# Two-layer mLSTM/convolution/MoE trunk: gate rows summed and rows spread by GpSimd, head norm weight as a column, layer 2's router loads and last modulation units moved

## The reference, cut to what matters

```
cond = silu(c)
for l in range(2):
    mod = cond @ w_ada[l] + b_ada[l]
    sh1, sc1, gt1, sh2, sc2, gt2 = split(mod, 6)
    u = x * (1 + sc1) + sh1
    proj = u @ w_in[l]                       # q k v o, gates, conv b c h
    h = mlstm_chunkwise(q, k, v, i_pre, f_pre)
    h = head_norm(h, mh_norm_w[l]) * sigmoid(o)
    y_conv = short_gated_conv(cb, cc, ch, w_conv[l])
    mix = concat([h, y_conv]) @ w_out[l]
    x = layer_norm(ALPHA * x + (1 + gt1) * mix, ln1_g[l], ln1_b[l])
    u = x * (1 + sc2) + sh2
    y = hier_moe(u, ...)                     # 16 experts in 4 groups, 2 per token
    x = layer_norm(ALPHA * x + (1 + gt2) * y, ln2_g[l], ln2_b[l])
```

## Time and profile before

| | us |
|---|---|
| median of 3 runs | 819.16 |
| lowest, highest | 817.65, 821.26 |
| profiled execution, its own time | 819.95 |
| its span, first to last instruction | 818.1 |

### The profile page before, as it was taken

One profiled execution on the slowest core, in us unless ns is written; L12 is line 12 of the kernel. 1 busy time (PEld: TensorE's weight loads), 2 busy tenths in 40 slices (PEclk: granted clock), 3 DMA queues, 4 the chain that ended last, 5 costly groups with the idle time before them and its releaser, 6 DMA issues.

```text
span 818.1 us, 9332 instructions
## 1 busy us (share of the span) xinstructions
PE 790.1 (97%) x3834; PEld 425.7 (52%) x3834; DVE 425.1 (52%) x916; ACT 96.0 (12%) x217; POOL 28.7 (4%) x72
## 2 busy tenths in 40 slices
PE   7999999999999999999979999999999999999994
PEld 2585588465344434434337658856634444443431
DVE  0289889787413332341356995676741343334135
ACT  2211000012011101101121101001201100110110
POOL 3000000520000000000001000000000000000000
PEclk9999999999999999999999999999999999999998
DMA  9999999899999999999998799547799999999991
GB/s 311 389 387 339 387 388 361 323 361 365 413 409 415 416 409 414 415 409 414 415 386 302 287 385 386 190 184 286 294 409 409 415 415 409 415 415 410 414 414 68
DMA packets 90826, 299.34 MB, mean 366 GB/s; under 512 B 4172, under 2 KB 4476, under 8 KB 82588
## 3 DMA queue, kind: packets, MB, share of 16 engines
q1 hardware_dynamic: 87132, 291.62, 91.7%
q0 software_dynamic: 2592, 7.04, 2.3%
q10 hardware_dynamic: 1056, 0.03, 0.1%
HBM read 297.63 MB, written 1.05 MB: 365 GB/s over the span
## 4 chain that ended last, share of the span: by engine, by line
PE 84%; DMA 6%; DVE 5%; issue 3%; ACT 1%; POOL 1%; DVEq 0%; POOLq 0%
PE bank L696 23%; PE bank L652 17%; PE bank L720 12%; PE bank L683 8%; PE bank L669 7%; DMA ring<-in_w_up_dram 6%; PE bank L742 4%; PE bank L889 3%; PE bank L536 2%; DVE bench L1141 1%; PE bank L551 1%; PE bank L568 1%; PE bank L704 1%; PE bank L750 1%; DVE expo L1141 1%
## 5 line engine op out<-in xcount | busy, mean ns | idle before, releaser
L652 PE MATMUL bank<-uT,ring 128*128 128x256 f32 x640 | 140.7, 380 | 0.0
L652 PEld LDWEIGHTS bank<-uT,ring 128*128 128x128 f32 x640 | 120.9, 190 | 19.3 <-issue 3.6
L696 PE MATMUL bank<-ring,uT 128*64 128x512 f32 x448 | 99.2, 594 | 1.8 <-DMA ring<-in_w_up_dram 1.8
L720 PE MATMUL bank<-ring,hb 128*64 128x512 f32 x448 | 99.6, 595 | 1.4 <-ACT hb L1012 1.4
L696 PE MATMUL bank<-ring,qT 128*64 128x512 f32 x448 | 99.4, 594 | 0.2 <-issue 0.2
L1141 DVE SCALAR_TENSOR_TENSOR bench<-ring,cond,bench 128x512 f32<-128x512 f32 x126 | 94.7, 752 | 4.5
L1376 DVE SCALAR_TENSOR_TENSOR kT<-bank,share,gate_row 128x512 f32<-128x512 f32 x32 | 24.0, 749 | 90.0 <-PE bank L720 90.0
L683 PEld LDWEIGHTS bank<-ccT,X 128*128 128x128 f32 x512 | 61.5, 197 | 11.3 <-issue 11.3
L696 PEld LDWEIGHTS bank<-ring,uT 128*64 128x64 f32 x448 | 31.6, 137 | 64.6 <-issue 60.0
L683 PE MATMUL bank<-ccT,X 128*128 128x128 f32 x512 | 64.3, 284 | 0.0
L720 PEld LDWEIGHTS bank<-ring,hb 128*64 128x64 f32 x448 | 30.9, 137 | 62.8 <-issue 60.5
(11 more groups left out here) (278 smaller groups left out, 658.5 us busy)
## 6 DMA issues: line engine op xcount, KB each, us to landing
ring<-in_w_gate_dram SPq DMA_DIRECT2D x28, 2048.0 KB, 18.5
ring<-in_w_up_dram SPq DMA_DIRECT2D x28, 2048.0 KB, 19.6
ring<-in_w_down_dram SPq DMA_DIRECT2D x28, 2048.0 KB, 16.9
ring<-in_w_ada_dram SPq DMA_DIRECT2D x23, 2048.0 KB, 18.2
ring<-in_w_in_dram SPq DMA_DIRECT2D x14, 2048.0 KB, 17.9
ring<-in_w_out_dram SPq DMA_DIRECT2D x4, 2048.0 KB, 15.5
bench<-in_w_gate_dram SPq DMA_DIRECT2D x4, 2048.0 KB, 11.9
bench<-in_w_up_dram SPq DMA_DIRECT2D x4, 2048.0 KB, 18.7
```

The costliest lines, as they stand in the source:

```text
L652: last = pe.matmul(bank[4 + (b0 + q) % 4][:, 0:SEQ], w[:, kc, q * P:(q + 1) * P], uT[:, kc, :], start=(kc == 0), stop=(kc == KC - 1))
L696: last = pe.matmul(bank[bk][CAP * j:CAP * (j + 1), :], xg[b][:, 4 * h + k, CAP * j:CAP * (j + 1)], ring[s[h]][:, 4 * j + k, :], start=(h = ...
L720: last = pe.matmul(bank[6 + half][CAP * j:CAP * (j + 1), :], hhT[:, f, CAP * j:CAP * (j + 1)], ring[s[h]][:, 4 * j + 2 * i + half, :], sta ...
```

## The change

- `gate_row_half`, `gate_rows` and `gate_row_2` are gone. DVE adds 1/128 on each partition when it weighs a gate unit, so that the sum over partitions has the 1 in it. GpSimd's new `gate_half` waits for the unit to be weighed, adds the bias row to partition 0 of the partial sums with an accumulating DMA of 2 KB, waits for it, and runs one `partition_all_reduce` of 128x512, which leaves the gate row on all partitions. Gate 2's row has a place of its own, `gate_moe`, over `v_ext`, whose columns of ones GpSimd writes again for layer 1 (PE waits for `ones_back`).
- `norm_rows` loads `ln_g` and `ln_b` to one partition (4 KB each) and spreads them with `partition_broadcast`; the router biases likewise. Layer 0's first norm rows are now loaded right after the constants.
- The head norm weight comes in with the convolution weights as columns (one more small DMA on SP, 16 instead of 12 columns transposed) and is applied by ACT as the scale of its copy of the transposed heads, in four instructions of 128x256 instead of two of 128x512; DVE's multiplication of 128x1024 is gone, and so is `mh_w`.
- PE runs `four_columns` after the first piece of the output projection; where gate 2's matmuls stood it runs `stay_busy(4, 4)`, four bf16 matmuls of zeros.
- Layer 1's router loads (ten DMAs) move from layer 0's output projection to after layer 1's `x_full`. In layer 1 units 10 and 11 are loaded before projections 5 and 6, and DVE weighs them in the middle of the mixer; it waits there for `gate_row_ready` at 4l+1 and 4l+2.
- The first load into `bench` waits for `moe_sum`, for `gate_row_ready` at 4l+4 and, in layer 0, for `early_sum`.

```diff
@@ STREAM[1]
-                  ("proj", 1, 3), ("ada", 1, 8), ("ada", 1, 9), ("proj", 1, 4), ("proj", 1, 5), ("proj", 1, 6), ("ada", 1, 10),
-                  ("ada", 1, 11), ("wout", 1, 0), ("wout", 1, 1)]
+                  ("proj", 1, 3), ("ada", 1, 8), ("ada", 1, 9), ("proj", 1, 4), ("ada", 1, 10), ("ada", 1, 11), ("proj", 1, 5),
+                  ("proj", 1, 6), ("wout", 1, 0), ("wout", 1, 1)]
@@ sync
-                            sp.wait_ge(row_ext, 4 * l + 4)
+                            sp.wait_ge(moe_sum, l + 1)
+                            sp.wait_ge(gate_row_ready, 4 * l + 4)
+                            if l == 0:
+                                sp.wait_ge(early_sum, 1)
@@ gpsimd
+            def gate_half(l, which, half):
+                i = (GATE1, GATE2)[which] + half
+                sums = weighed_sums(l, i)
+                bias = b_ada[l, ADA_COL[i]:ADA_COL[i] + COLS].rearrange("(a n) -> a n", a=1)
+                pool.wait_ge(weighed, turn(l, i))
+                pool.dma_start(sums[0:1, :], bias, accum_op=ALU.add).then_inc(bias_added, 16)
+                pool.wait_ge(bias_added, 16 * (4 * l + 2 * which + half + 1))
+                row = (gate_row, gate_moe)[which]
+                pool.partition_all_reduce(row[:, half * COLS:(half + 1) * COLS], sums, P,
+                                          bass.bass_isa.ReduceOp.add).then_inc(gate_row_ready, 1)
...
             for l in range(DEPTH):
                 if l:
                     pool.wait_ge(x_full, l)
-                arrived(pool, "proj", l, 4 if l == 0 else 1)
-                load_gate_row(l, 0)
-                load_head_weight(l)
+                    pool.memset(v_ext[:, :, :, DK:DK + 1], 1.0).then_inc(ones_back, 1)
+                    load_route(l)
+                norm_rows(l, 0)
+                for half in range(2):
+                    gate_half(l, 0, half)
                 if l == 0:
                     arrived(pool, "wout", l, 1)
-                load_norm_rows(l, 0)
-                if l == 0:
-                    for i in range(DEPTH):
-                        load_route(i)
-                    for i in range(1, DEPTH):
-                        load_gates(pool, i)
-                pool.wait_ge(x_ready, 2 * T * l + T)
-                load_gate_row(l, 1)
+                    load_route(l)
+                    load_gates(pool, 1)
+                pool.wait_ge(route_landed, 16 * 10 * (l + 1))
+                pool.partition_broadcast(b_route_row[:, l, :], b_route_row[0:1, l, :], channels=P).then_inc(route_spread, 1)
+                pool.wait_ge(pv_done, HEADS * (l + 1))
+                for half in range(2):
+                    gate_half(l, 1, half)
                 pool.wait_ge(seeded, l + 1)
-                load_norm_rows(l, 1)
+                norm_rows(l, 1)
@@ vector
-                link(dve.tensor_tensor(hb[:, :, :], hb[:, :, :], mh_w[:, :].unsqueeze(1).to_broadcast([P, T, WM]), ALU.mult))
                 dve.tensor_tensor(hb[:, :, :], hb[:, :, :], o_sig[:, :, :], ALU.mult).then_inc(h_ready, 1)
...
-                gate_rows(l, 0)
-                for i in (GATE2, GATE2 + 1):
-                    dve.wait_ge(row_ext, 4 * l + 2)
-                    ada_weigh(l, i)
-                    if i == GATE2:
-                        moe_shift_scale(l)
                 dve.wait_ge(gate_row_ready, 4 * l + 2)
+                if l == 0:
+                    ada_weigh(l, GATE2)
+                moe_shift_scale(l)
+                if l == 0:
+                    ada_weigh(l, GATE2 + 1)
                 first_norm(l)
```

114 lines of the change are left out of this document (51 added, 63 removed).

## The result

The changed kernel takes **827.7 us** (median of 4 runs, 827.1 to 833.3) where the kernel before took 819.7 beside it: 1.0094 of its time, 95% interval 1.0061 to 1.0126. Forecast were 814.4 us and "faster", so the sign is wrong. The time lies inside the range, but through a cause that the range wasn't built on. The profiled execution has a span of 826.5 us, against 818.1: 8.4 us to find.

The account below looks back on a forecast made before the run. PE, with work for 97% of the span, was taken as the bound, the DMA weight stream close behind. Savings 1.8 + 0.95 + 0.2 + 1.8 = 4.75 us gave 814.4 us; range for 8 in 10: 812.5 to 830.

Parts of the forecast that it names:

- PE, gate 1's matmuls, -1.8: Output projection, layer 1: gate 1's matmuls go and four transposes move behind the first piece, saving 1.8 us.
- DVE, layer 0, -0.95: Layer 0's output projection: DVE loses the gate rows but waits 2 us for transposed sums, saving 0.95 us, not 3.
- rival 3: Layer 0's norm and routing: GpSimd's sums stretch DVE by a fifth, 2 to 3 us, giving 817 us; chance 0.08.
- PE, gate 2's matmuls, -0.1 a layer: Gate 2 on PE: four zero matmuls of about 1 us replace matmuls whose second lasts 1.10; saves 0.1 us a layer.
- DMA, -1.8: Expert weight stream: two row loads a layer go, so PE's two waits for the last up loads go, saving 1.8 us.
- the margin of 1.5 us: Expert weight stream: what is left of the DMA saving after PE's two waits are gone, 1.5 us.
- Costs at nothing: Head weight, extra small DMA, early norm rows, GpSimd code loading and layer 1's moved units: each priced at no loss.
- The new cost, GpSimd's sums: Gate sums and bias DMAs on GpSimd: layer 0's first `bench` load is free at 189.0, in time before 191.4.
- X = 5.1 us: GpSimd's time for one 128x512 sum over partitions, taken as a halving tree of eight passes of 0.64 us.
- Rivals 1, 2 and 4: Stream waits for GpSimd, 825.8 us (0.24); part comes back, about 819 (0.22); sums far slower, about 1135 (0.03).
- the sum's 4.75 us: Whole kernel: total saving forecast, 1.8 + 0.95 + 0.2 + 1.8 us.

Follow-up runs that it names:

- a_pe2_late: a_back with layer 1's first norm rows spread later and gate 2 summed by PE, not GpSimd, and copied by ACT: 817.4 us (0.9955).
- a_back: The changed kernel with one iota of four numbers at the end of GpSimd's stream: 819.4 us (0.9999 of the kernel before).
- a_pe2_fill: a_pe2_late with layer 1's norm rows back in place and eight filler matmuls on PE ending layer 0's experts: 815.7 us (0.9920).
- b_fill: The kernel before with eight filler matmuls on PE at the end of layer 0's experts, nothing else: 819.2 us (0.9972).
- b_sums: The kernel before with four unused GpSimd sums of a dead tile in layer 0 and an iota ending GpSimd's stream: 826.8 us (1.0061).
- b_spread: The kernel before with one unused row of four numbers spread over the partitions at the end of GpSimd's stream: 832.0 us (1.0163).

## Why the prediction was wrong

Point by point, in its own order:

- *PE, gate 1's matmuls, -1.8*: right. Layer 1's mixer went from 118.49 to 116.78, -1.71, both at full clock; in four later profiles of the changed family a clock dip takes it back.
- *DVE, layer 0, -0.95*: the mechanism right, with the wait for the transposes at 2.00 us where 2 were forecast, and the size right (-0.89 in a_pe2_late). In the changed kernel it did not come, since rival 3, given 0.08, stood in its place: DVE's operations beside GpSimd's sums. Rival 3 was thought of as a stretch by a fifth over 16 us. It is a hold of up to 2 us at a time on operations between SBUF tiles that start beside a sum: here 1.3 us ahead of X's first norm, and 0.5 us behind it. "Layer 0: -0.95 us" became +0.44.
- *PE, gate 2's matmuls, -0.1 a layer*: -0.25 in layer 0 and 0 in layer 1 (from X's first norm to the first `share`, 35.79 to 35.54 and 35.61 to 35.61). The 35.54 has a clock dip in it, 188 to 192, where PE waits for DVE; a_back has 35.49 without one.
- *DMA, -1.8*: the mechanism right, the size nearer to -1.1. In the changed kernel's own profile the last pair of layer 0 begins 1.24 us earlier behind the one ahead of it (25.38 to 24.14), that of layer 1 0.48 (25.16 to 24.68), together -1.7. But that profile is one of the two best of its family. PE's two waits for the last up load together are 1.6 to 1.9 us in the six profiles of the kernel before's family (mean 1.75) and 0.25 to 1.3 in the eight of the changed family (mean 0.7). So they shrink and don't go, and the margin of 1.5 us that the prediction saw behind them isn't there. On the way to softmax 1 the changed kernel then loses 0.8 us, with PE idle for 4.46 us instead of 4.07 and a longer dip of the clock behind it.
- *Costs at nothing*: **this is the step that failed.** The prediction put "the code that GpSimd's new operations may have to load" at nothing, since "GpSimd is free from 8 us". That prices the load where the new operations stand, and there it does cost nothing (6.63 us of idle time, hidden). The load that costs, if that is what the idle time is, is that of the old operations: the constants' code, which the kernel before always found in place. It costs 10.46 us ahead of PE's first matmul with a constant, and all behind it is as late. In the profile of before nothing shows it, because that kernel holds operations of one kind; what was left out is that a profile shows one execution in a row of them.
- *The new cost, GpSimd's sums*: X = 5.1 us was too high, 3.24 measured, and the bias DMA 5.2 to 5.4 instead of 6.2; both harmless. Rivals 1, 2 and 4 fell with it: no wait of the stream for GpSimd was found. The 62 us for 512 columns that the rate in the Trainium skill, page "GPSIMD Engine Reference", section 3.2, would give are 19 times what this operation takes.

With the start put right (a_back) the changed kernel equals the one before, and with gate 2's sums away from DVE as well (a_pe2_late) it is 0.45% faster. What stays open is how much of that, a_pe2_fill over b_fill included, is the sum's 4.75 us: the rows give 0.9 + 1.7 + 0.2 + 1.1 = 3.9 us, the medians 3.6 (a_pe2_fill against b_fill) and 3.8 (a_pe2_late against the kernel before). That the forecast range held the measured 827.7 is luck: it reached that far for a stream that waits for GpSimd, and the stream didn't.

## What to carry to other kernels

Ask of a GpSimd operation of a new kind not only what it costs where it stands, but what it leaves loaded for the next execution: here one unused row at the end of the stream cost 1.6%, and one iota behind it gave that back. Put GpSimd's work on SBUF where DVE idles or reads PSUM, not where DVE is the engine that ends last; a sum that is off the path itself can still hold DVE's instructions that are on it. And where savings of a microsecond are at stake, compare stretch by stretch, with the granted clock beside each, since a dip of the clock is as large as any of them.

## What the runs showed of the hardware that I had not expected

- GpSimd's change of kind (a load of code, as inferred above): 10.6 to 10.7 us of idle time ahead of the first select of an execution whose kernel ends with a partition operation; 10.9 to 12.9 us ahead of an iota behind a partition operation; 6.1 us (b_sums) to 9.8 us (a_pe2_late) ahead of the first partition operation. Memsets and DMA issues between the two kinds run at once and don't bring it on (b_sums).
- `partition_all_reduce` of 128x512 takes 3.24 us (up to 3.8 beside DVE's weighing), `partition_broadcast` of 128x1024 1.30 us. Beside the start of a sum, a DVE operation of 0.31 us between SBUF tiles took 2.02 us, one of 0.81 us 2.70, one of a single column 0.76 for 0.22; reads of PSUM were not delayed.
- Behind 4.1 us without a matmul PE got clocks of 0.74 and 0.69 in two slices of 3 us. Behind 1.8 us (a_back) it kept 1.00, behind 1.96 us (b_spread) it got 0.69 and 0.74. The low clock alone cost b_spread's way to the next softmax 0.6 us; PE's late return from its idle stretch is put at 2.3 us in the kernel before. Eight filler matmuls removed both.
